# Sparse attention by query tile, with the selection of a tile's keys in rounds between the attention steps of the tile before it

## What is computed

```python
act = relu(einsum("bqhd,bsd->bqhs", qi, k_idx) * IDX_DIM ** -0.5)      # 8 index heads
score = einsum("bqh,bqhs->bqs", wi, act)
score = where(cid[None, :] <= cid_q[:, None], score, NEG_INF)
_, sel = lax.top_k(score, k_sel)                                       # k_sel = 128
kv = gather(c_kv, sel)
logits = einsum("bqhr,bqkr->bqhk", qa, kv) * B_KV_RANK ** -0.5 + bias  # 16 heads, rank 256
p = softmax(where(valid, logits, NEG_INF))
o_lat = einsum("bqhk,bqkr->bqhr", p, kv)
o = einsum("bqhr,hrd->bqhd", o_lat, w_uv)
```

## Time and profile before

| | us |
|---|---|
| median of three runs | 4351.23 (4349.64 to 4355.53) |
| the profiled execution, its own time | 4350.4 |
| its span, first to last instruction | 4348.7 |
| TensorE busy in the span | 3892.5 (90%) |
| VectorE busy | 1699.1 (39%) |
| ScalarE busy | 1253.9 (29%) |
| the first half of `latent_heads`, from its first index product to its last column sums | 1732.3 to 1893.3 |
| its second half, up to the output projection | 1893.3 to 2174.1 |

### The profile page before, as it was taken

The page is one execution under the profiler, slowest core; times in us unless marked ns, Lnnn a source line. Parts: engine busy times, 40 slices in busy tenths (PEclk is TensorE's granted clock), DMA queues, the critical chain, the costliest instruction groups (busy, mean ns, idle before and its releaser), DMA issues. The chain is left out here.

```text
span 4348.7 us, 52492 instructions
## 1 busy us (share of the span) xinstructions
PE 3892.5 (90%) x20782; PEld 3070.7 (71%) x20782; DVE 1699.1 (39%) x2622; ACT 1253.9 (29%) x1775; POOL 228.3 (5%) x217
## 2 busy tenths in 40 slices
PE   8999787799999998588899999998997886799998
PEld 7998666699999994255558888884344664446886
DVE  4432556344344322543334434434771111124432
ACT  4321455333233311243324324421001111103431
POOL 0000211000000000010000000000730000000000
PEclk9999898799999998699999999999998886799999
DMA  4322211122222222000022232221112001113221
GB/s 168 119 82 85 87 44 35 39 90 91 80 98 91 82 68 84 15 27 1 1 88 96 91 102 97 93 93 60 44 44 80 22 0 39 54 62 106 96 84 71
DMA packets 87268, 305.36 MB, mean 70 GB/s; under 512 B 8343, under 2 KB 35095, under 8 KB 70004
## 3 DMA queue, kind: packets, MB, share of 16 engines
q1 hardware_dynamic: 87156, 303.90, 20.1%
HBM read 301.66 MB, written 10.72 MB: 72 GB/s over the span
## 5 line engine op out<-in xcount | busy, mean ns | idle before, releaser
L323 PE MATMUL acc<-fb_xh,fb_wh 128*128 128x264 f32 x1408 | 287.9, 286 | 12.4 <-DVE fb_wl L473 12.4
L323 PE MATMUL acc<-fb_xl,fb_wh 128*128 128x264 f32 x1408 | 288.2, 286 | 0.0
L323 PE MATMUL acc<-fb_xh,fb_wl 128*128 128x264 f32 x1408 | 287.7, 286 | 0.0
L323 PE MATMUL acc<-fd_xh,fd_wh 128*128 128x512 f32 x704 | 275.8, 392 | 10.4 <-DVE fd_wl L473 10.4
L323 PE MATMUL acc<-fd_xl,fd_wh 128*128 128x512 f32 x704 | 274.8, 390 | 0.0
L323 PE MATMUL acc<-fd_xh,fd_wl 128*128 128x512 f32 x704 | 274.8, 390 | 0.0
L323 PEld LDWEIGHTS acc<-fb_xh,fb_wh 128*128 128x128 f32 x1408 | 220.1, 189 | 12.8 <-DVE fb_wl L473 12.6
L323 PEld LDWEIGHTS acc<-fb_xl,fb_wh 128*128 128x128 f32 x1408 | 219.4, 189 | 0.0
L323 PEld LDWEIGHTS acc<-fb_xh,fb_wl 128*128 128x128 f32 x1408 | 219.0, 189 | 0.0
L394 ACT ACTIVATE fb_wh<-fb_raw 128x2048 fp32r<-128x2048 f32 (+1 forms) x74 | 124.9, 1687 | 289.9 <-PE acc L382 176.9
L468 DVE TENSOR_TENSOR fb_wl<-fb_raw,fb_wh 128x2048 fp32r<-128x2048 f32 (+1 forms) x74 | 148.3, 2005 | 141.4 <-ACT fb_wh L394 140.6
(11 more groups left out here) (504 smaller groups left out, 8456.9 us busy)
## 6 DMA issues: line engine op xcount, KB each, us to landing
fb_raw<-wi_dram SPq DMA_DIRECT2D x42, 1024.0 KB, 4.8
fd_raw<-wi_dram SPq DMA_DIRECT2D x42, 1024.0 KB, 4.8
fb_raw<-wo_dram SPq DMA_DIRECT2D x32, 704.0 KB, 4.0
fd_raw<-wo_dram SPq DMA_DIRECT2D x32, 704.0 KB, 4.0
fa_raw<-wi_dram SPq DMA_DIRECT2D x20, 1024.0 KB, 4.8
ff_raw<-wi_dram SPq DMA_DIRECT2D x20, 1024.0 KB, 4.8
a_raw<-a_qkv_dram SPq DMA_DIRECT2D x24, 512.0 KB, 4.1
s_gw<-gate_w_dram SPq DMA_DIRECT2D x24, 512.0 KB, 3.3
```

Source lines behind the costliest of these rows:

```text
L323: last = pe.matmul(acc[:, up_base(p, b) + 2 * a + q, 0:w], x[:, k, a, :], part[:, k, t0:t0 + w], start=k == 0 and part is xh and x is wv, ...
```

## The change

The steps go tile by tile: 16 heads with tile 0, then 16 with tile 1, and so on. Places that took a step's tile from `g % NT` now look it up, and the output projection waits for the last 16 steps in pairs. The selection is put into two functions, `pick` (one round) and `visible` (the final mask). In the first half only tile 0 still has its selection, as a loop. The selections of tiles 1 to 3 run in the second half, written out: behind `logit(g + 2)` of a step of tile `t`, VectorE runs one round for tile `t + 1` (two for heads 6 and 13; heads 14 and 15 have none), and after the sixteenth, in head 13, the final mask. The masking of the later chunk before the selection stays where it was, in the first half.

```diff
-            STEPS_ = [(hd, t) for hd in range(B_HEADS) for t in range(NT)]
+            STEPS_ = [(hd, t) for t in range(NT) for hd in range(B_HEADS)]
...
                     def turn(g):
-                        keys = REAL_TILES[g % NT][2]
+                        keys = REAL_TILES[STEPS_[g][1]][2]
...
                             if c == 0:
-                                pe.wait_ge(mixed, 1 + 2 * NT * (k + 1))
+                                pe.wait_ge(mixed, 1 + B_HEADS * (NT - 1) + 2 * (k + 1))
...
                 @block.vector
                 def _(dve):
+                    def pick(i):
+
+                        score = mb[:, i, 0:META + (i + 1) * P]
+                        dve.max(top8[:, :], score)
+                        dve.drain()
+                        dve.match_replace(out=score, in_to_replace=top8[:, :], in_values=score, imm_value=TAKEN)
+                        dve.drain()
+
+                    def visible(i):
+
+                        keys = META + (i + 1) * P
+                        dve.tensor_scalar(mb[:, i, 0:keys], mb[:, i, 0:keys], TAKEN / 1.5, MASKED, ALU.is_gt, ALU.mult)
+                        dve.drain()
+                        dve.memset(mb[0:CHUNK, i, keys - CHUNK:keys], MASKED)
+                        dve.drain()
+
...
                         dve.memset(mb[0:CHUNK, i, keys - CHUNK:keys], MASKED)
                         dve.drain()
-                        with dve.Fori(0, TOPK // 8):
-                            dve.max(top8[:, :], score)
-                            dve.drain()
-                            dve.match_replace(out=score, in_to_replace=top8[:, :], in_values=score, imm_value=TAKEN)
-                            dve.drain()
-                        dve.tensor_scalar(score, score, TAKEN / 1.5, MASKED, ALU.is_gt, ALU.mult)
-                        dve.drain()
-                        dve.memset(mb[0:CHUNK, i, keys - CHUNK:keys], MASKED)
-                        dve.drain()
+                        if i == 0:
+                            with dve.Fori(0, TOPK // 8):
+                                pick(0)
+                            visible(0)
...
+                    PICKS, LAST_PICK = TOPK // 8, B_HEADS - 3
                     for g in range(LAST):
+                        hd, t = STEPS_[g]
                         weigh(g)
                         if g + 2 < LAST:
                             logit(g + 2)
+                        if t + 1 < NT and hd <= LAST_PICK:
+                            for _ in range((hd + 1) * PICKS // (LAST_PICK + 1) - hd * PICKS // (LAST_PICK + 1)):
+                                pick(t + 1)
+                            if hd == LAST_PICK:
+                                visible(t + 1)
```

More of the change, by code:

```diff
@@ L1643, in _ @@
                 def _(dve):
+                    def pick(i):
[10 more added lines that the diff above has]
+                        dve.drain()
                     for n, (i, hd, a, b) in enumerate(jobs):
                         keys = META + (i + 1) * P
-                        score = mb[:, i, 0:keys]
                         dve.wait_ge(relued, 1 + n + 1)
```

## The result

The changed kernel takes 4431.5 us (median of four, 4425.4 to 4437.2), the kernel before 4350.4: a ratio of 1.0186, interval 1.0167 to 1.0204. It is slower by 81 us, 1.9%; 4419 was forecast, in a range of 4368 to 4458.

What follows compares the result with a forecast made beforehand. First half: TensorE waits through unhidden selections; second half: a closed chain of steps with no engine full. 4350.4 - 46 (first half) + 69 (rounds, masks) + 49 (clock) - 3 (old slow start) = 4419.4 us, range 4368 to 4458.

Steps and rivals of the forecast that it cites:

- the mechanism of the chain: Second half: turn, scores, logit and diagonal form a closed chain, so a round behind the logit lengthens it fully.
- rounds and masks in the chain: Second-half steps: 48 rounds at 66.9 us plus three final masks at 2, together 69 us added.
- clock, less the slow start of before: Second-half steps: 49 us for TensorE at half clock, less 3 us its slow start already cost.
- Part 1: First half: three selections leave it, so it ends at 1847.3 instead of 1893.3, a gain of 46.0 us.
- Part 2: Second half: 48 unrolled rounds of 1.13, 1.39 and 1.66 us enter the steps' chain; with masks 69 us.
- Rival 3: Second half: rounds fit into VectorE's idle time, so the kernel gets faster, 4306 us; chance 0.04.
- its point of decision: Rounds hide once TensorE's outputs (0.8 to 1.45 us) exceed logit rest, round and diagonal (at least 2.4).
- Part 3: Second half: going tile by tile leaves the steps' sum the same, 2.83, 3.74, 4.65 and 5.86 us a step.
- Part 4: Second-half steps: TensorE falls to half clock for tile 0, partly for tiles 1 and 2, costing 49 us.
- the half taken for tiles 1 and 2: Steps of tiles 1 and 2: clock comes and goes, so half of each one's half-clock cost, 32.7 us.
- rival 1: Second half: TensorE's clock stays at 2.4 GHz through the steps, 4370 us; chance 0.13.
- Rivals 1 and 2: TensorE's clock in the steps: 2.4 GHz throughout, 4370 us, chance 0.13; or 1.2 GHz for tiles 0 to 2, 4452, 0.19.

Runs made afterwards that it cites:

- tile 3 back: The changed kernel with tile 3's selection back in the first half, rounds for tiles 1 and 2 still behind the logit: 4386.2 us.
- clock kept: The changed kernel with two extra 256-column TensorE products behind the outputs in steps of tiles 0 to 2, rounds still behind the logit: 4394.6 us.
- order only: The kernel before with only the steps reordered tile by tile; all four selections stay in the first half as loops: 4369.2 us.
- the round before the logit: The changed kernel with each round moved from behind logit(g+2) to between weigh(g) and logit(g+2): 4326.7 us.
- wake once: The changed kernel with rounds ahead of the logit, tile 0's selection behind all additions, and two extra TensorE products in steps 1 to 4: 4310.2 us.
- wake and hold: The changed kernel, rounds ahead of the logit, tile 0's selection behind all additions, two extra products in steps 1 to 4, one in tile 0's others: 4298.6 us.

## Why the prediction was right

The signs and the mechanism of the chain held; part of the clock's cost was put down to the wrong cause. The forecast was 12 us low by the medians. In the profiles the two halves lose 83 us for a forecast 69: the first half gained 5 less and the clock cost 11 more, the rounds cost 1 less. Another 4 us lie in untouched stages.

| term | forecast | measured |
|---|---|---|
| first half | -46 | -41.4 (160.2 to 118.8) |
| rounds and masks in the chain | +69 | +68 |
| clock, less the slow start of before | +46 | +57 |

- **Part 1, first half.** 41.4 us, within its bounds of 39 to 50. Nearly 3 of the missing 5 lie ahead of tile 0's selection: first query to selection took 18.0 us at clock 0.75, before 15.3. No edit is there, and other kernels with this first half show one value or the other (15.4 in tile 3 back); TensorE's granted clock there was 0.75, before 0.89. From the selection on the gain is 44.2. The rest of the miss is the four heads with products, 7.8 us each (1780.5 to 1811.7) for the 7.3 taken.
- **Part 2, rounds.** Full-clock steps with a round against full-clock steps without: 5.11 - 3.74 and 6.29 - 4.66 in clock kept and order only; at half clock 5.02 - 3.92. That is 1.10, 1.37, 1.63 for the forecast 1.13, 1.39, 1.66, 66 for the 48, and 2 for masks. The 0.35 us of idle ahead of each pass of the loop did vanish. That place, not quantity, makes the price is shown by the round before the logit. Rival 3 was rightly set low for the kernel as changed, but its mechanism is real, and its point of decision was the order of two calls.
- **Part 3, order.** The chain's sum came out as worked out, 2.83, 3.74, 4.66, 5.88 in runs at full clock. "The sum is the same" failed for the clock, see next.
- **Part 4, clock.** The size was near, in part by luck: tile 0 is at half clock with or without rounds, and the half taken for tiles 1 and 2 was a guess. I had tile 0 fall because of the rounds. Order only shows it at half clock with none: the clock falls where the first half ends, before the first turn, in the kernel before as well (windows, columns as in rows 1):

```profile
1892.30:1893.30 1.00, 0.92 (x9) 0.93 (x9) 0.00 (x0) 0.00 (x0) 0.02 (x1) 1.00 0.00 0
1893.30:1896.20 2.90, 2.87 (x10) 1.86 (x9) 1.46 (x5) 2.05 (x4) 0.00 (x0) 0.54 0.59 215
```

  Just ahead of that TensorE makes column sums of one column and waits 1.67 us for GpSimd between them; whether this brings the fall wasn't tried. Tile 0's steps, gathered together, then never lift it. Before, larger steps came in between, and it was back within 14 us. So 18.5 us belong to the order. For tiles 1 and 2, the steps at full clock would be 61.2 and 76.6 us, with rounds and masks 83.8 and 103.4; they took 103.7 and 125.2, 20 and 22 of clock. Forecast 13.6 and 19.1. Order only had 3.5 of tile 1's already, so 18.5 + 16 + 22 = 57.
- **Two slips in the working.** The stage of the earlier trace rows was counted among those whose pauses stay under 2 to 3 us. Its trace has one of 3.02 us again and again, so it says less against rival 1 than was made of it:

```profile
3503.57 1.54 PE L2210 MATMUL acc<-ident,d_e 128*128 128x128 f32 x6 [3.02 <-DVE d_e L2271]
```

  And a quarter to nine tenths of 65.3 us of clock, with 5 us on either side, is 4398 to 4450, not 4392 to 4440; the measured time lies in both.
- **Rivals 1 and 2.** Both fall by the clock column: 0.65 and 0.77, neither 1.00 nor 0.50. The steps of tile 0 in order only stay at 0.50 with TensorE busy 63.66 of 68.5 us and no pause over 1.45 us. In wake once the clock even fell, from 0.99 to 0.51, behind 9.4 us of which TensorE was busy 8.01, with no pause over 1.12 us. The Trainium skill ("TensorE: Matmul & The Clock Gate", "Why this matters for your kernels") names long idle gaps between bursts as what to avoid against a drop in mid-kernel; the trace shows that in this stage avoiding them isn't enough. Busy time also stretches with the slower clock, so a high busy share at 0.50 isn't a sign of dense work.

What stays open: why within tile 1 the changed kernel's steps with one round first vary between 5.1 and 6.8 us and then stay at 6.83, with no change in the program. Tile 3 back shows much the same course, so it isn't chance alone; its cause wasn't tried. Nor was it tried what at the end of the first half takes the clock down.

## What to carry to other kernels

Idle time on an engine is usable only at the point of its program where it idles: find the wait, and put the extra work directly ahead of it; a few lines further down the same work can cost its full length. Before moving work, look which part of it is free already (here the last selection) and leave that. And if TensorE loses its clock at a stage's border, what comes first behind it matters: here 16 small steps in a row kept it low. Filling their pauses with one spare product each brought 8 us; beginning with larger steps, as the kernel before does, wasn't tried by itself.

## What the runs showed of the hardware that was not expected

- Tile 0's steps stay at 0.50 for all 16 if they begin there (order only). Raised by extra products (wake once) they had 0.99 for 9.4 us, the last 5.6 without such products, and then 0.51 again. With one extra product of 256 columns in each (wake and hold) they kept 1.00, at no cost to the step (2.83 us).
- Adding 94 useless products to TensorE made the kernel 37 us faster than the change without them (4394.6 for 4431.5).
- An unrolled selection round on 272 keys costs its two passes and 0.24 us around them (1.10 us in all); in the loop it was 0.50.
